# A first stage in another order: x turned before it is modulated, and half of the modulation sums on TensorE

## The chip, the cores and the metric

One core of a Trainium2 chip. The time is the device time of one execution in microseconds (us); of several runs the median is given. The engines are called PE (TensorE; PEld its weight loads), DVE (VectorE), ACT (ScalarE), POOL (GpSimd) and SP (SyncE, which only issues transfers).

## The reference

A transformer block for 1024 tokens of width 1024, all float32. What matters here is its beginning:

```python
c_act = jax.nn.silu(c)
mod = c_act @ w_mod[l] + b_mod[l]
sh1, sc1, gt1, sh2, sc2, gt2 = jnp.split(mod, 6, axis=-1)
h = modulate(rmsnorm(x, g_mix[l]), sh1, sc1)      # rmsnorm(x)*g * (1 + sc1) + sh1
x = x + gt1[:, None, :] * token_mixers(h, cos, sin, w_in[l], ...)
h = modulate(rmsnorm(x, g_ffn[l]), sh2, sc2)
x = x + gt2[:, None, :] * hier_moe(h, ...)
```

w_mod is 1024 x 6144, so each of the six vectors is the product of silu(c), 1024 numbers, with a 1024 x 1024 piece (4 MB). The token mixers begin with h @ w_in; then come an indexer, two kinds of attention, and a mixture of 32 experts, which read 6 MB of weights each.

## The kernel before

The kernel is written as five programs, one per engine, which wait for one another by semaphores; the order on each engine is the order of its program. x is kept as eight tiles xs[t] of 128 tokens x 1024. The projections need it the other way round: hT[kt] holds 128 channels x 1024 tokens, kt = 0 to 7, normalized and modulated.

The first stage runs as follows. SP asks for five small vectors (L448 to L452: c, b_mod, g_mix, positions, b_forget, all counted by the semaphore c_in), for the first two 2 MB pieces of w_mod (L454), for the eight tiles of x (L456), then, as buffers come free, for two more pieces of w_mod (L459), for the narrow columns of w_in (L462, wsmall) and 512 wide ones (L464, wqi). DVE waits for c_in, prepares the angles of the rotary embedding (L1290 to L1305), makes sil = silu(c), and takes the sums of w_mod: `mod_sums(n)` adds up, for the 512 columns n, the eight row blocks times sil (L1317 and L1319, eight instructions), which leaves 128 partial sums per column in acc. ACT squares and sums each tile of x (L718), takes the root of all sums at once (L720), DVE scales the eight tiles (L1332). PE turns x by transposes (L950), four to a PSUM bank, sixteen banks in all, seven of them before it needs one back. After the seventh it makes the sums over the partitions: 16 products of a 128 x 128 piece of acc with one column of ones (L956), which give shift and scale, one column of PSUM for each 128 channels. DVE adds b_mod and g_mix (L1337 to L1339: sh1, a1). Only then can a bank leave PSUM: ACT and DVE take the banks in turn and apply a1 and sh1 on the way (L729, L1351). When all sixteen are out, PE projects tile after tile (`project`: L966, 208 columns, then L971, 512 columns) and DVE takes the eight remaining `mod_sums`, one after each tile's rotary embedding.

Each float32 product stands in the trace as two matmul instructions; a transpose is one. POOL fills the constants first (invf, wm, ident, upper, ones; L605 to L616), the semaphores freq_ok and consts; PE waits for consts, DVE for freq_ok.

## Time and profile before

| | us |
|---|---|
| runs (3) | 1920.46, 1921.70, 1925.42 |
| median | 1921.7 |
| the profiled execution, its own time | 1920.38 |
| its span | 1918.1 |
| PE busy | 1682.2 |
| DVE busy | 983.1 |
| ACT busy | 494.1 |
| POOL busy | 193.8 |

The span runs from the first to the last instruction of the profiled execution; 2.3 us of its own time lie around it. Mean granted clock of PE is 0.957 of full speed. In the rows below, "idle before" names what ended an engine's wait; PEclk of 1.00 is 2.4 GHz, of 0.50 is 1.2 GHz; a DMA share of 1.0 means that all sixteen DMA engines were busy.

### The profile page before, as it was taken

The page shows a single profiled execution, that of the slowest core. Times are in us where ns is not written, and L with a number is a line of the kernel's source. Part 1 is how long each engine was busy: PE and PEld are TensorE (multiplying, and loading weights), DVE is VectorE, ACT ScalarE, POOL GpSimd, SP SyncE. Part 2 cuts the span into 40 slices and gives each one's busy share as a digit, 9 for nine tenths or more (in the row PEclk, how much of TensorE's full clock was granted, in tenths as well). Part 3 has the DMA queues.
Part 4 walks back from the last instruction along what each step waited for, and adds up shares of the span by engine and source line. Part 5 has one row for each costly group of instructions (what it writes and reads, how often), then busy time and mean ns, then how long its engine had stood idle before and what let it go on. Part 6 is the DMA issues. An engine that isn't in the chain of part 4 may idle for free.

```text
span 1918.1 us, 22810 instructions
## 1 busy us (share of the span) xinstructions
PE 1682.2 (88%) x7893; PEld 868.9 (45%) x7894; DVE 983.1 (51%) x1928; ACT 494.1 (26%) x976; POOL 193.8 (10%) x370
## 2 busy tenths in 40 slices
PE   1997899999998886999999995799888999899991
PEld 0662366565544453676665553333222333333330
DVE  6477558888887564556555435223222233233334
ACT  2116254554545563110110111111111111111112
POOL 0010000000000000000000000122211222222220
PEclk9898999999999998999999997799998999999996
DMA  8552311010001002112114516599999973779967
GB/s 281 187 208 77 142 35 45 23 44 1 1 1 56 1 1 66 34 33 66 33 33 162 225 66 248 195 394 391 405 405 405 400 270 61 268 271 397 355 223 279
DMA packets 114582, 325.52 MB, mean 170 GB/s; under 512 B 15240, under 2 KB 53128, under 8 KB 89936
## 3 DMA queue, kind: packets, MB, share of 16 engines
q1 hardware_dynamic: 102768, 296.79, 40.8%
q0 software_dynamic: 11744, 27.79, 6.1%
q8 instruction: 44, 0.72, 0.2%
q14 instruction: 26, 0.21, 0.0%
HBM read 293.33 MB, written 31.23 MB: 169 GB/s over the span
## 4 chain that ended last, share of the span: by engine, by line
PE 76%; DVE 8%; DMA 8%; ACT 4%; issue 3%; SPq 1%; DVEq 0%; ACTq 0%; POOLq 0%; POOL 0%
PE ps L1216 17%; PE ps L1156 9%; PE ps L1234 8%; PE ps L1017 6%; PE ps L1145 6%; PE ps L1170 5%; DMA arena<-in_w_e_up_dram 5%; PE ps L1042 3%; PE ps L1023 3%; PE ps L1093 3%; PE ps L971 3%; PE ps L1067 3%; PE ps L1053 2%; DVE arena L1401 2%; PE ps L1210 2%
## 5 line engine op out<-in xcount | busy, mean ns | idle before, releaser
L1216 PE MATMUL ps<-arena 128*64 128x512 f32 x1632 | 387.0, 618 | 39.1 <-DMA arena<-in_w_e_up_dram 27.6
L1743 DVE COPY arena<-ps 128x256 f32<-128x256 f32 x51 | 21.6, 424 | 425.5 <-ACT arena L902 425.5
L1216 PEld LDWEIGHTS ps<-arena 128*64 128x64 f32 x1632 | 118.5, 141 | 261.6 <-issue 254.5
L1234 PE MATMUL ps<-arena 128*64 128x512 f32 x816 | 186.3, 598 | 0.5 <-ACT arena L906 0.5
L1156 PE MATMUL ps<-rounded 128*128 128x512 f32 x768 | 183.3, 398 | 0.0
L1419 DVE TENSOR_SCALAR_CACHE_REDUCE arena<-arena,small 128x384 bf16<-128x384 f32 (+2 forms) x204 | 182.0, 939 | 0.0
L1156 PEld LDWEIGHTS ps<-rounded 128*128 128x128 f32 x768 | 144.3, 188 | 36.5 <-issue 7.7
L703 POOL DMA_INDIRECT sum_rows<-arena,ones x51 | 81.4, 1595 | 467.9 <-DVE arena L1765 459.1
L1145 PE MATMUL ps<-arena 128*128 128x512 f32 x256 | 115.3, 604 | 13.2 <-DVEq L1589 13.2
L1017 PE MATMUL ps<-arena 128*128 128x512 f32 x256 | 116.7, 610 | 4.8 <-ACT arena L766 3.4
L1067 PE MATMUL ps<-arena 128*64 128x128 f32 x1152 | 96.1, 287 | 26.3 <-ACT arena L800 22.8
L906 ACT ACTIVATE arena<-ps 128x256 f32<-128x256 f32 x51 | 19.5, 383 | 371.9 <-PE ps L1225 371.9
L1482 DVE CUSTOM_DVE_ANT_0 arena<-ps,arena 128x896 f32<-128x896 f32 (+7 forms) x128 | 91.7, 753 | 46.0 <-PE ps L1042 45.9
L1170 PE MATMUL ps<-arena 128*128 128x512 f32 x256 | 112.0, 595 | 2.0 <-DMA arena<-in_w_out_dram 2.0
L800 ACT ACTIVATE arena<-ps 128x512 f32<-128x512 f32 (+1 forms) x160 | 85.1, 551 | 84.3 <-PE ps L1053 83.8
L1595 DVE RECIPROCAL arena<-arena 128x1024 f32<-128x1024 f32 x16 | 104.8, 6553 | 0.5
L787 ACT ACTIVATE arena<-arena,small 128x896 f32<-128x896 f32 (+7 forms) x128 | 97.8, 768 | 19.9 <-DVE small L1482 19.9
L1234 PEld LDWEIGHTS ps<-arena 128*64 128x64 f32 x816 | 54.2, 136 | 93.9 <-issue 87.9
L1067 PEld LDWEIGHTS ps<-arena 128*64 128x64 f32 x1152 | 60.0, 136 | 74.0 <-ACT arena L800 45.9
L1042 PE MATMUL ps<-arena 64*128 64x512 f32 (+3 forms) x384 | 80.8, 526 | 12.3 <-DVE small L1482 11.6
L1053 PE MATMUL ps<-ident,arena 128*128 128x128 f32 x576 | 89.0, 287 | 0.0
L1748 DVE RECIPROCAL arena<-arena 128x256 f32<-128x256 f32 x51 | 89.0, 1745 | 0.0
(267 smaller groups left out, 1915.4 us busy)
## 6 DMA issues: line engine op xcount, KB each, us to landing
arena<-in_w_e_gate_dram SPq DMA_DIRECT2D x32, 2048.0 KB, 15.0
arena<-in_w_e_up_dram SPq DMA_DIRECT2D x32, 2048.0 KB, 20.1
arena<-in_w_e_down_dram SPq DMA_DIRECT2D x32, 2048.0 KB, 15.6
arena<-in_w_mod_dram SPq DMA_DIRECT2D x12, 2048.0 KB, 8.9
arena<-in_w_in_dram SPq DMA_DIRECT2D x33, 512.0 KB, 4.6
arena<-in_x_dram SPq DMA_DIRECT2D x16, 512.0 KB, 12.3
arena<-sum_rows SPq DMA_DIRECT2D x16, 512.0 KB, 10.6
sum_rows<-arena SPq DMA_DIRECT2D x2, 2304.0 KB, 16.5
```

The costliest lines, as they stand in the source:

```text
L787: act.activation(buf, buf, ACT.Exp, bias=nmax[:, u:u + 1], scale=-1.0, accum_out=rs[:, u:u + 1]).then_inc(p_done, 1)
L1017: m = pe.matmul(ps[:, 7, :], wB[j][:, kt, :], hT[:, kt, half * 512:(half + 1) * 512], start=kt == 0, stop=kt == KT - 1)
L1042: m = pe.matmul(ps[:, 2 * z + a // 512, 0:e - a], q[half, b * P:(b + 1) * P], k[half, a:e], start=True, stop=True)
L1053: m = pe.transpose(ps[:, 4 + k % 2, (2 * i + z) * P:(2 * i + z + 1) * P], logits(n)[z][:, kb * P:(kb + 1) * P], ident[:])
L1067: m = pe.matmul(ps[z * HD:(z + 1) * HD, 6, 0:P], v, pT_of(n, g)[:, (2 * i + z) * P:(2 * i + z + 1) * P], start=kb == 0, stop=kb == b)
L1145: m = pe.matmul(ps[:, 4 * half + 2 + g, :], w[2 + g][:, kt, :], oT[g][kt][:, tok], start=kt == 0, stop=kt == 3)
L1156: m = pe.matmul(ps[:, 4 * half + g, :], a, b, start=kt == 0 and k == 0, stop=kt == KT - 1 and k == 2)
L1170: m = pe.matmul(ps[:, 2 * (t % 2) + n, :], mT[:, kt, t * P:(t + 1) * P], wout[:, kt, n * 512:(n + 1) * 512], start=kt == 0, stop=kt == KT - 1)
L1216: m = pe.matmul(ps[o * TB:(o + 1) * TB, 2, 0:2 * FQ].rearrange("p (j n) -> p j n", j=2), xT[:, k % NX, k // NX * TB:(k // NX + 1) * TB], w ...
L1234: m = pe.matmul(ps[o * TB:(o + 1) * TB, 5, 0:DQ], hidT[:, k % NH_T, k // NH_T * TB:(k // NH_T + 1) * TB], w_dn[c][:, k, o * DQ:(o + 1) * D ...
L1419: chain.up(dve.tensor_scalar(junk[b % 2][:, 0:WB[B0 + b]], scb[b], thr(b), None, op, ALU.add, accum_out=cnt[:, b:b + 1]))
L1595: link(dve.reciprocal(e, e))
```

## The change

The five small vectors are asked for by POOL, ahead of its constants, and no longer by SP. SP asks for x first, then for all four pieces of w_mod (four buffers instead of two, so no waits), then for wsmall and wqi. ACT and DVE take x tile by tile: square, mean, root, reciprocal, scaling; PE turns each scaled tile (eight transposes in two banks), and ACT and DVE copy the two banks to hT without modulation. After the last tile ACT takes the exponential for sil. The sums for n = 1 and 3 stay on DVE; those for n = 0 and 2 are made by PE alone, as products of w_mod's 128 x 128 pieces with the column sil[kt], eight to a sum. With sh1 and a1 known, ACT (kt = 0, 3, 6) and DVE (the others) modulate hT in place, and PE's first projection waits for one kt after the other. The counts of acc_ok fall by two everywhere, and mod2's first loads wait for modp_ok too.

```diff
         xs = at(37, 8 * U, [TT, D])
-        wslot = [at(8, 4 * U, [KT, 512]), at(12, 4 * U, [KT, 512])]
+        mod1 = [at(u, 4 * U, [KT, 512]) for u in (16, 21, 25, 30)]
         wsmall = at(8, KT * P_N, [KT, P_N])
-        wqi = wslot[1]
+        wqi = at(12, 4 * U, [KT, 512])
+        sq_out = [at(45 + z, U) for z in range(2)]
         acc = [at(49, U), at(50, U)] + [at(45 + j, U) for j in range(4)]
...
         def _(sp):
-            sp.dma_start(cT, c.rearrange("o (t p) -> p (o t)", p=P), allow_slow_non_contiguous=True).then_inc(c_in, 16)
-            sp.dma_start(bmod, b_mod[0, 0:2 * D].rearrange("(t p) -> p t", p=P), allow_slow_non_contiguous=True).then_inc(c_in, 16)
-            sp.dma_start(gmix, g_mix[0].rearrange("(t p) -> p t", p=P), allow_slow_non_contiguous=True).then_inc(c_in, 16)
-            sp.dma_start(posi, positions[0].rearrange("(t p) -> p t", p=P), allow_slow_non_contiguous=True).then_inc(c_in, 16)
-            sp.dma_start(bfb, b_forget[0:1, :].to_broadcast([P, NH])).then_inc(c_in, 16)
-            for n in range(2):
-                sp.dma_start(wslot[n], w_mod_v[:, :, n * 512:(n + 1) * 512]).then_inc(mod_in[n], 16)
             for t in range(TT):
                 sp.dma_start(xs[:, t, :], x_v[t]).then_inc(x_in[t], 16)
-            for n in range(2, 4):
-                sp.wait_ge(acc_ok, n - 1)
-                sp.dma_start(wslot[n % 2], w_mod_v[:, :, n * 512:(n + 1) * 512]).then_inc(mod_in[n % 2], 16)
-            sp.wait_ge(acc_ok, 3)
+            for n in range(4):
+                sp.dma_start(mod1[n], w_mod_v[:, :, n * 512:(n + 1) * 512]).then_inc(mod_in[n], 16)
             for a, b, n in ((C_KI, P_KI, 72), (C_KA, P_KA, 128), (C_F, P_F, NH)):
                 sp.dma_start(wsmall[:, :, b:b + n], w_in_v[:, :, a:a + n], allow_slow_non_contiguous=True).then_inc(wi_in[0], 16)
-            sp.wait_ge(acc_ok, 4)
             sp.dma_start(wqi, w_in_v[:, :, C_QI:C_QI + 512]).then_inc(wi_in[1], 16)
             sp.wait_ge(xt_ps, 16)
+            sp.wait_ge(modp_ok, 1)
             for n in range(4, 12):
                 if n >= 6:
-                    sp.wait_ge(acc_ok, n - 1)
+                    sp.wait_ge(acc_ok, n - 3)
                 sp.dma_start(mod2[n % 2], w_mod_v[:, :, n * 512:(n + 1) * 512]).then_inc(mod_in[n % 2], 16)
...
                 if j == 2:
-                    sp.wait_ge(acc_ok, 12)
+                    sp.wait_ge(acc_ok, 10)
                 sp.dma_start(wB[j], w_in_v[:, :, (C_QB, C_KB, C_VB)[j]:(C_QB, C_KB, C_VB)[j] + P]).then_inc(wb_in[j], 16)
...
 
+            pool.dma_start(cT, c.rearrange("o (t p) -> p (o t)", p=P), allow_slow_non_contiguous=True).then_inc(c_in, 16)
+            pool.dma_start(posi, positions[0].rearrange("(t p) -> p t", p=P), allow_slow_non_contiguous=True).then_inc(c_in, 16)
+            pool.dma_start(bmod, b_mod[0, 0:2 * D].rearrange("(t p) -> p t", p=P), allow_slow_non_contiguous=True).then_inc(c_in, 16)
+            pool.dma_start(gmix, g_mix[0].rearrange("(t p) -> p t", p=P), allow_slow_non_contiguous=True).then_inc(c_in, 16)
+            pool.dma_start(bfb, b_forget[0:1, :].to_broadcast([P, NH])).then_inc(c_in, 16)
             for j in range(HALF):
...
         def _(act):
-            act.wait_ge(c_in, 80)
-            act.activation(sil, cT, ACT.Exp, scale=-1.0).then_inc(silu_e, 1)
-            for t in range(TT):
+            def square(t):
                 act.wait_ge(x_in[t], 16)
                 if t >= 2:
                     act.wait_ge(ssq_ok, t - 1)
-                act.activation(relu[t % 2], xs[:, t, :], ACT.Square, accum_out=ssq[:, t:t + 1]).then_inc(ssq_ok, 1)
-            act.wait_ge(ms_ok, 1)
-            act.activation(rstd, ssq, ACT.Sqrt).then_inc(sqrt_ok, 1)
+                act.activation(sq_out[t % 2], xs[:, t, :], ACT.Square, accum_out=ssq[:, t:t + 1]).then_inc(ssq_ok, 1)
+
+            def turned_x(t):
+                act.wait_ge(xt_ps, 2 * t + 1)
+                act.activation(hT[:, 0:4, t * P:(t + 1) * P], ps[:, 2 * t % 6, :].rearrange("p (j m) -> p j m", j=4), ACT.Copy).then_inc(xt_act, 1)
+
+            square(0)
+            for t in range(TT):
+                if t + 1 < TT:
+                    square(t + 1)
+                act.wait_ge(ms_ok, t + 1)
+                act.activation(rstd[:, t:t + 1], ssq[:, t:t + 1], ACT.Sqrt).then_inc(sqrt_ok, 1)
+                if t >= 1:
+                    turned_x(t - 1)
+            turned_x(TT - 1)
+            act.wait_ge(c_in, 80)
+            act.activation(sil, cT, ACT.Exp, scale=-1.0).then_inc(silu_e, 1)
             act.wait_ge(ang_ok, 1)
...
             act.wait_ge(mod1_ok, 2)
-            for n in range(0, 16, 2):
-                act.wait_ge(xt_ps, n + 1)
-                kt, half = n // 2, n % 2
-                act.activation(hT[:, kt, half * 512:(half + 1) * 512], ps[:, n % 7, :], ACT.Identity,
-                               bias=sh1[:, kt:kt + 1], scale=a1[:, kt:kt + 1]).then_inc(xt_act, 1)
+            act.wait_ge(xt_dve, TT)
+            for kt in (0, 3, 6):
+                act.activation(hT[:, kt, :], hT[:, kt, :], ACT.Identity, bias=sh1[:, kt:kt + 1], scale=a1[:, kt:kt + 1]).then_inc(xt_act, 1)
 
...
                 pe.wait_ge(xn_ok, t + 1)
-            for n in range(16):
-                kt, half = n // 2, n % 2
-                if n >= 7:
-                    pe.wait_ge(xt_act if (n - 7) % 2 == 0 else xt_dve, (n - 7) // 2 + 1)
-                for j in range(4):
-                    t = 4 * half + j
-                    m = pe.transpose(ps[:, n % 7, j * P:(j + 1) * P], xs[:, t, kt * P:(kt + 1) * P], ident[:])
-                m.then_inc(xt_ps, 1)
-                if n == 6:
-
-                    pe.wait_ge(acc_ok, 4)
-                    for k in range(2 * KT):
-                        m = pe.matmul(ps[:, 7, k:k + 1], acc[k // KT][:, (k % KT) * P:(k % KT + 1) * P], ones[:, 0:1],
-                                      start=True, stop=True)
-                    m.then_inc(modp_ok, 1)
-            pe.wait_ge(xt_act, 8)
-            pe.wait_ge(xt_dve, 8)
+                for h in range(2):
+                    if t >= 3:
+                        pe.wait_ge((xt_act, xt_dve)[h], t - 2)
+                    for j in range(4):
+                        kt = 4 * h + j
+                        m = pe.transpose(ps[:, (2 * t + h) % 6, j * P:(j + 1) * P], xs[:, t, kt * P:(kt + 1) * P], ident[:])
+                    m.then_inc(xt_ps, 1)
+
+            pe.wait_ge(sil_ok, 1)
+            for n in (0, 2):
+                pe.wait_ge(mod_in[n], 16)
+                for k in range(4 * n, 4 * n + 4):
+                    for kt in range(KT):
+                        m = pe.matmul(ps[:, 7, k:k + 1], mod1[n][:, kt, k % 4 * P:(k % 4 + 1) * P], sil[:, kt:kt + 1],
+                                      start=kt == 0, stop=kt == KT - 1)
+            for n in (1, 3):
+                pe.wait_ge(acc_ok, 1 + n // 2)
+                for k in range(4 * n, 4 * n + 4):
+                    m = pe.matmul(ps[:, 7, k:k + 1], acc[k // KT][:, (k % KT) * P:(k % KT + 1) * P], ones[:, 0:1], start=True, stop=True)
+            m.then_inc(modp_ok, 1)
 
...
                 for kt in range(KT):
+                    if t == 0 and kt % 3 == 0:
+                        pe.wait_ge(xt_act, TT + 1 + kt // 3)
+                    elif t == 0:
+                        pe.wait_ge(xt_dve, TT + kt - kt // 3)
                     pe.matmul(ps[:, t % 2, 0:P_N], hT[:, kt, t * P:(t + 1) * P], wsmall[:, kt, :],
...
 
-            dve.wait_ge(silu_e, 1)
-            link(dve.tensor_scalar(sil, sil, 1.0, None, ALU.add))
-            link(dve.reciprocal(sil, sil))
-            link(dve.tensor_tensor(sil, sil, cT, ALU.mult))
-
             def mod_sums(n):
 
-                w = wslot[n % 2] if n < 4 else mod2[n % 2]
-                dve.wait_ge(mod_in[n % 2], 16 * (n // 2 + 1))
+                w = mod1[n] if n < 4 else mod2[n % 2]
+                dve.wait_ge(mod_in[n if n < 4 else n % 2], 16 if n < 4 else 16 * ((n - 4) // 2 + 2))
                 a = acc[n // 2][:, (n % 2) * 512:(n % 2 + 1) * 512]
...
 
-            mod_sums(0)
+            def turned_x(t):
+                dve.wait_ge(xt_ps, 2 * t + 2)
+                dve.tensor_copy(hT[:, 4:8, t * P:(t + 1) * P], ps[:, (2 * t + 1) % 6, :].rearrange("p (j m) -> p j m", j=4)).then_inc(xt_dve, 1)
+
+            def mean(t):
+                dve.wait_ge(ssq_ok, t + 1)
+                dve.tensor_scalar(ssq[:, t:t + 1], ssq[:, t:t + 1], 1.0 / D, EPS, ALU.mult, ALU.add).then_inc(ms_ok, 1)
+
+            mean(0)
+            for t in range(TT):
+                if t + 1 < TT:
+                    mean(t + 1)
+                dve.wait_ge(sqrt_ok, t + 1)
+                link(dve.reciprocal(rstd[:, t:t + 1], rstd[:, t:t + 1]))
+                dve.tensor_scalar(xs[:, t, :], xs[:, t, :], rstd[:, t:t + 1], None, ALU.mult).then_inc(xn_ok, 1)
+                if t >= 1:
+                    turned_x(t - 1)
+            dve.wait_ge(silu_e, 1)
+            link(dve.tensor_scalar(sil, sil, 1.0, None, ALU.add))
+            link(dve.reciprocal(sil, sil))
+            dve.tensor_tensor(sil, sil, cT, ALU.mult).then_inc(sil_ok, 1)
+            turned_x(TT - 1)
+            dve.wait_ge(sil_ok, 1)
             mod_sums(1)
-
-            dve.wait_ge(ssq_ok, TT)
-            dve.tensor_scalar(ssq, ssq, 1.0 / D, EPS, ALU.mult, ALU.add).then_inc(ms_ok, 1)
-            dve.wait_ge(sqrt_ok, 1)
-            link(dve.reciprocal(rstd, rstd))
-            for t in range(TT):
-                dve.tensor_scalar(xs[:, t, :], xs[:, t, :], rstd[:, t:t + 1], None, ALU.mult).then_inc(xn_ok, 1)
-            mod_sums(2)
             mod_sums(3)
...
             dve.scalar_tensor_tensor(a1, a1, 1.0, gmix, ALU.add, ALU.mult).then_inc(mod1_ok, 1)
+
+            dve.wait_ge(mod1_ok, 2)
+            dve.wait_ge(xt_act, TT)
+            for kt in range(KT):
+                if kt % 3:
+                    dve.tensor_scalar(hT[:, kt, :], hT[:, kt, :], a1[:, kt:kt + 1], sh1[:, kt:kt + 1], ALU.mult, ALU.add).then_inc(xt_dve, 1)
 
...
             link(dve.tensor_copy(cos2[:, :, 1, :], cos2[:, :, 0, :]))
-
-            dve.wait_ge(mod1_ok, 2)
-            for n in range(1, 16, 2):
-                dve.wait_ge(xt_ps, n + 1)
-                kt, half = n // 2, n % 2
-                dve.tensor_scalar(hT[:, kt, half * 512:(half + 1) * 512], ps[:, n % 7, :], a1[:, kt:kt + 1],
-                                  sh1[:, kt:kt + 1], ALU.mult, ALU.add).then_inc(xt_dve, 1)
 
```

Left out are the declarations of semaphores and three more places where a wait for acc_ok 12 becomes one for 10.

On POOL, at the start of its program: these rows stood there before (small is where invf and wm lie).

```order
L605 MEMSET small 128x1 x8
L607 MEMSET small 128x1 x6
L609 MEMSET ident 128x128
L610 MEMSET upper 128x128
L611 MEMSET ones 128x128
L614 ISA [waits pool_chain]
L614 AFFINE_SELECT ident<-ident 128x128
L616 AFFINE_SELECT upper<-upper 128x128
```

And these stand there now, with the five transfers ahead of the constants.

```order
L596 DMA small<-in_c_dram 128x8x1
L597 DMA small<-in_positions_dram 128x8x1
L598 DMA small<-in_b_mod_dram 128x16x1
L599 DMA small<-in_g_mix_dram 128x8x1
L600 DMA small<-in_b_forget_dram 128x8
L602 MEMSET small 128x1 x8
L604 MEMSET small 128x1 x6
L606 MEMSET ident 128x128
L607 MEMSET upper 128x128
L608 MEMSET ones 128x128
L611 ISA [waits pool_chain]
L611 AFFINE_SELECT ident<-ident 128x128
```

Everything that POOL does in this stage has moved behind the transfers: freq_ok, for which DVE waits, and consts, for which PE waits.

On DVE, from the last angle step on, before (ssq, rstd and sil lie in small, xs, acc and the buffers of w_mod in arena):

```order
L1305 TENSOR_SCALAR arena<-arena 128x64 [waits dve_chain]
L1308 TENSOR_SCALAR small<-small 128x8 [waits silu_e]
L1309 RECIPROCAL small<-small 128x8 [waits dve_chain]
L1310 TENSOR_TENSOR small<-small 128x8 [waits dve_chain]
L1317 TENSOR_SCALAR arena<-arena,small 128x512 [waits mod_in0,dve_chain]
L1319 SCALAR_TENSOR_TENSOR arena<-arena,small 128x512 [waits dve_chain] x7
L1317 TENSOR_SCALAR arena<-arena,small 128x512 [waits mod_in1]
L1319 SCALAR_TENSOR_TENSOR arena<-arena,small 128x512 [waits dve_chain] x7
L1328 TENSOR_SCALAR small<-small 128x8 [waits ssq_ok]
L1330 RECIPROCAL small<-small 128x8 [waits sqrt_ok]
L1332 TENSOR_SCALAR arena<-arena,small 128x1024 [waits dve_chain]
L1332 TENSOR_SCALAR arena<-arena,small 128x1024 x7
```

And now:

```order
L1319 TENSOR_SCALAR arena<-arena 128x64 [waits dve_chain]
L1339 TENSOR_SCALAR small<-small 128x1 [waits ssq_ok] x2
L1346 RECIPROCAL small<-small 128x1 [waits sqrt_ok]
L1347 TENSOR_SCALAR arena<-arena,small 128x1024 [waits dve_chain]
L1339 TENSOR_SCALAR small<-small 128x1 [waits ssq_ok]
L1346 RECIPROCAL small<-small 128x1 [waits sqrt_ok]
L1347 TENSOR_SCALAR arena<-arena,small 128x1024 [waits dve_chain]
L1335 COPY arena<-ps 128x4x128 [waits xt_ps]
L1339 TENSOR_SCALAR small<-small 128x1 [waits ssq_ok]
L1346 RECIPROCAL small<-small 128x1 [waits sqrt_ok]
```

The scaling of the first tile comes right behind the angles instead of behind two sums, in rounds of a tile each; sil has moved behind the eighth tile.

On PE, from the last transposes of x to the last one-column product, now (small is sil, ps the PSUM):

```order
L956 MATMUL ps<-ident,arena 128x128 [waits xt_act,xn_ok]
L956 MATMUL ps<-ident,arena 128x128 x3
L956 MATMUL ps<-ident,arena 128x128 [waits xt_dve]
L956 MATMUL ps<-ident,arena 128x128 x3
L964 MATMUL ps<-small,arena 128x1 [waits mod_in0,sil_ok]
L964 MATMUL ps<-small,arena 128x1 x31
L964 MATMUL ps<-small,arena 128x1 [waits mod_in2]
L964 MATMUL ps<-small,arena 128x1 x31
L969 MATMUL ps<-ones,arena 128x1 [waits acc_ok]
L969 MATMUL ps<-ones,arena 128x1 x3
L969 MATMUL ps<-ones,arena 128x1 [waits acc_ok]
L969 MATMUL ps<-ones,arena 128x1 x3
```

Of these L964 is new, 64 products; of L969's kind there were 16 and are 8.

## Rows read from the trace of the kernel before

**Rows 1.** The page: busy time by engine, and the chain's shares by engine.

```profile
PE 1682.2 (88%) x7893; PEld 868.9 (45%) x7894; DVE 983.1 (51%) x1928; ACT 494.1 (26%) x976; POOL 193.8 (10%) x370
...
PE 76%; DVE 8%; DMA 8%; ACT 4%; issue 3%; SPq 1%; DVEq 0%; ACTq 0%; POOLq 0%; POOL 0%
```

**Rows 2.** The chain that ended last, 0 to 150 us: start, us, what.

```profile
14.53 14.84 DMA arena<-in_x_dram
...
49.60 7.00 PE ps L956 x32
...
57.93 5.51 PE ps L950 x32
...
64.82 3.05 PE ps L966 x16
67.87 6.87 PE ps L971 x16
```

**Rows 3.** Stretches: us, busy (instructions) of PE, PEld, DVE, ACT, POOL, clock, DMA share, GB/s.

```profile
20.00:30.00 10.00, 0.00 (x0) 0.00 (x0) 5.48 (x8) 8.65 (x15) 0.00 (x0) 1.00 1.03 406
43.00:48.00 5.00, 0.00 (x0) 0.00 (x0) 4.79 (x7) 0.00 (x0) 0.00 (x0) 1.00 0.72 168
50.00:56.00 6.00, 6.00 (x29) 6.00 (x30) 0.00 (x0) 0.00 (x0) 0.00 (x0) 0.50 0.90 318
57.00:61.00 4.00, 3.07 (x15) 3.04 (x16) 3.87 (x10) 3.56 (x5) 0.00 (x0) 0.50 0.00 0
62.00:63.00 1.00, 1.00 (x12) 1.00 (x10) 0.81 (x1) 0.83 (x2) 0.00 (x0) 1.00 0.00 0
1166.00:1168.00 2.00, 2.00 (x20) 1.98 (x18) 1.38 (x2) 0.33 (x1) 0.00 (x0) 1.00 0.00 0
1178.00:1181.00 3.00, 3.00 (x16) 3.00 (x15) 0.00 (x0) 0.00 (x0) 0.00 (x0) 0.50 1.02 434
```

**Rows 4.** Timeline of DVE, 0 to 63 us: start, us, engine, line, operation, idle before.

```profile
7.88 0.17 DVE L1290 CAST small<-small 128x8 f32<-128x8 int32 x1 [7.88 <-DMA small<-in_b_forget_dram]
...
10.52 0.20 DVE L1305 TENSOR_SCALAR arena<-arena 128x64 f32<-128x64 f32 x1
...
32.34 5.39 DVE L1332 TENSOR_SCALAR arena<-arena,small 128x1024 f32<-128x1024 f32 x8
...
38.16 5.47 DVE L1319 SCALAR_TENSOR_TENSOR arena<-arena,small 128x512 f32<-128x512 f32 x7
...
57.81 3.79 DVE L1351 TENSOR_SCALAR arena<-ps,small 128x512 f32<-128x512 f32 x5
```

**Rows 5.** Timeline of SP's queue, 0 to 5 us.

```profile
4.58 0.89 SPq L452 DMA_DIRECT2D small<-in_b_forget_dram  x1
```

**Rows 6.** Timeline of ACT, 20 to 76 us.

```profile
20.43 1.06 ACT L718 ACTIVATE arena<-arena 128x1024 f32<-128x1024 f32 x1 [12.35 <-DMA arena<-in_x_dram]
...
21.71 1.06 ACT L718 ACTIVATE arena<-arena 128x1024 f32<-128x1024 f32 x1
...
30.57 1.28 ACT L720 ACT_TABLE_LOAD   x1
31.86 0.21 ACT L720 ACTIVATE small<-small 128x8 f32<-128x8 f32 x1
...
75.07 0.59 ACT L741 ACTIVATE arena<-ps 128x512 f32<-128x512 f32 x1
```

**Rows 7.** Timeline of PE: the first transposes, and router products about 1170 us.

```profile
37.88 4.84 PE L950 MATMUL ps<-ident,arena 128*128 128x128 f32 x28 [37.88 <-DVE arena L1332]
...
1166.89 1.87 PE L1188 MATMUL ps<-arena 128*128 128x36 f32 x16
...
1173.84 3.47 PE L1188 MATMUL ps<-arena 128*128 128x36 f32 x16
```

**Rows 8.** A group on POOL, shapes apart: xcount, busy, mean ns, idle before.

```profile
L673 POOL DMA_INDIRECT arena<-h_rows,ones x55 | 55.5, 1009 | 43.6 <-POOL ones L670 43.6
```

**Rows 9.** Source line L673: its transfers from issue to landing.

```profile
DMA to landing us min/median/max: 3.4/8.6/10.6
```

10 lines of the change are left out of this document (5 added, 5 removed).

## The prediction

> **What bounds the kernel now.** The page comes first: TensorE (PE) is busy 88% of the span and carries 76% of the chain that ended last [rows 1]. A share over the whole span does not say what ends this stage, so the second view is that chain in order of time [rows 2]. It reads: the load of x (14.84 us) to 29.4 us, the eight scalings of x on VectorE (DVE) and two modulation sums there [rows 4], at 49.60 us sixteen one-column products on PE (7.0 us, 32 instructions), the last transposes, and at 64.82 us the first projection: 3.05 us of 208-column and 6.87 us of 512-column products, over at 74.74 us. Before 64.82 us nobody can project; after it PE works tile after tile, and what follows hangs on that end. So the time of this change is the shift of 74.74 us, one for one: I know of no slack behind it that would absorb a shift, since the later weight loads are issued by events of the same chain. The third view is the stretches with the granted clock [rows 3], then come the timelines of DVE, SP, ACT and PE, and the groups of POOL's own transfers.
>
> **What goes.** x no longer stands behind 4 MB of w_mod and does not wait for the sums; the 16 transposes of a half need no modulation vector. Two of the four sums leave DVE. All 12.6 MB of x and w_mod plus 2.9 MB of w_in are now asked for without a wait: at 406 GB/s [rows 3] that is 38 us, so mod1[3] is in by about 36 us and w_in by 44 us (with some 4 us of latency). Each is in before it is needed below, so these loads cost nothing; the cover is the PE work that runs until after 60 us.
>
> **What comes, step by step.** Call t the time at which the five small vectors (c_in) have landed. It was 7.88 us [rows 4], the last having been issued by SP at 4.58 us [rows 5].
>
> 1. DVE waits for t ahead of everything, as before, and its angle work takes 2.8 us (7.88 to 10.72) [rows 4]. In the old order this stood beside loads. Now the scaling of tile 0 is queued behind it, and PE's first transpose waits for that. The tile loop starts at t + 2.8.
>
> 2. The loop is bounded by ScalarE (ACT), which per tile does a square (1.28 us from one to the next), a root (0.2) and a copy of 512 columns from PSUM (0.6) [rows 6], with about 0.1 for handing over: 2.2 us. DVE has two small steps of 0.2, a scaling of 0.7 (5.39/8) and a copy from PSUM of 0.8 (3.79/5) = 1.9 us per tile [rows 4] and PE eight transposes of at most 0.17 us (5.51/32) [rows 2] = 1.4 us, so both hide beside ACT. x comes at 1.3 us a tile and hides too. Seven rounds are 15.4 us, the last tile's own scaling, transposes and copy 0.7 + 0.6 + 0.6 = 1.9 us: 17.3 us. ACT then loads a table (1.28) and takes the exponential (0.2) [rows 6]; DVE's three small steps are 0.6 us. So sil is ready at t + 2.8 + 17.3 + 1.5 + 0.6 = **t + 22.2**.
>
> 3. PE now makes 64 one-column products from w_mod itself (for n = 0 and 2) and 8 from the two sums left: 72 products, 144 instructions. The 32 of before took 7.0 us, 219 ns each [rows 2], at the lower of the clock's two levels, 0.50 = 1.2 GHz [rows 3]. 144 x 0.219 = **31.5 us**, where 7.0 stood. A weight load per product sets this pace: router products of 36 columns take 3.47/16 = 217 ns at the lower level and 1.87/16 = 117 ns at 1.00, 2.4 GHz [rows 3, 7]. So the bounds are 16.8 us and 31.5 us. I take 31.5: in the stretch 50 to 56 us the clock stood at 0.50 although PE was busy with such products all the time, and again at 1178 to 1181 us with 36 columns, whereas transposes from 57.93 us on brought it to 1.00 by 62 us [rows 2, 3]. DVE's two sums (6 us each, 5.47 us of it for the seven longer steps [rows 4]) hide beside the first 28 us.
>
> 4. From the last product to the first projection: 0.5 us for the two vectors, 1.1 us for ACT's first 1024-wide modulation, as its square is [rows 6]. The other seven pieces are ready at 0.7 to 1.1 us steps while PE works. The first projection then starts at the lower clock. Transposes needed about 4 us to bring it up (57.93 to 62) [rows 2, 3], so about 2 us are lost on the 9.9. Together 0.5 + 1.1 + 9.9 + 2.0 = **13.5 us**; before, 56.6 to 74.74 was 18.1 us.
>
> Sum: the first projection ends at t + 22.2 + 31.5 + 13.5 = t + 67.2. Against 74.74 the change is **t - 7.5 us**. Even with the old t = 7.88 nothing is gained: the early transposes are paid back by the one-column products. The outcome now hangs on t, at one for one.
>
> **How large t is.** The five vectors leave SP for POOL's queue. c, positions, b_mod and g_mix go as single 4-byte elements: 1024, 1024, 2048 and 1024 of them; last comes b_forget with 128 rows. The trace of before has no direct transfer from POOL. The nearest row is the gather of L673: 1.0 us of POOL for 128 rows [rows 8]. Lower bound: 1.0 us each, so 4.0 us ahead of the last. Upper bound: the cost grows with the elements, 1009/128 = 7.9 ns each, x 5120 = 40 us. I take 2.0 us each, 8 us, nearer the lower end, since a good part of 1009 ns must be fixed. From issue to landing a gather takes 3.4 us at best and 8.6 in the median [rows 9], the latter with SP's weight loads beside it; SP's x and w_mod are beside it here, so 8.6. With POOL's start at 0.8 us, t = 0.8 + 8 + 8.6 = 17.4 us, and the change is 17.4 - 7.5 = **+9.9 us**. The memsets of ident and ones also stand behind these transfers on POOL, but they end before t + 2.8 and cost nothing then. The profiled execution took 1920.4 us, 1.3 us under the median of 1921.7; the shift is the same for both, so I forecast 1921.7 + 9.9 = 1931.6 us.
>
> **Rivals.** *Quick landing (0.24).* Each transfer takes POOL 1.0 us and lands in 3.4 us: t = 0.8 + 4.0 + 3.4 = 8.2 us, the change is +0.7 us, 1922.4 us. Everything with t under 13.3 us belongs here, since 0.3% (5.8 us), about what a measurement of this kernel can tell from no change, is reached at that t. For it: 3.4 us occurs in the trace [rows 9]. Against it: the engines move 400 GB/s from 8 us on [rows 3]. The Trainium skill, "DMA: Bandwidth & Descriptors", section on the anatomy of a transfer from POOL, puts a transfer at about 2.0 us plus its bytes at 436 GB/s; by that, an estimate, t would be some 7 us and the change about -0.5 us.
>
> *Elements are dear (0.14).* 7.9 ns for each of 5120 elements gives t = 0.8 + 40 + 8.6 = 49 us and +42 us, 1964 us; if small pieces instead take turns with SP's rows on the engines until SP's 38 us of loads are through, t is about 40 us and the change +33 us. For it: each vector is all single elements, 5120 pieces in all where a gather has 128. The rules at the end of the same page of the skill say that a strided last dimension costs a descriptor per element. No row here shows what POOL pays for one.
>
> *The other side: the clock holds (0.10).* If PE's clock is up after the transposes and the one-column products keep it, they cost 16.8 us instead of 31.5, and the 2.0 us at the projection go too: -16.7, with t = 17.4 a change of -6.8 us, 1914.9 us. It becomes faster than before once more than 9.9/16.7 = 60% of that comes. For it: the clock stood at 1.00 until 48 us although the transposes had stopped at 42.7 us [rows 3, 7]. Against it: 7 us of the same products without a rise, and about 3 us lie between the last transpose and the first product. What I grant is some us of full clock at the start, up to 4.5 us (5 us hold 43 instructions at 117 ns, which else take 9.4).
>
> **How the numbers follow.** Forecast, t from 13.3 to 34 us: 0.52, likeliest 1931.6 us. The range runs from the quick landing with up to 4.5 us of clock, 1922.4 - 4.5 = 1918, to 1948 us, where t is 34 us (four transfers of 6 us); that leaves out most of the dear elements and the fully held clock, about 0.2. Slower by over 0.3%: 0.52 + 0.14, less 0.04 in which a partly held clock brings it under = 0.62. Within: 0.24 + 0.04 - 0.01 = 0.27. Faster: 0.10 plus 0.01 of the quick landing with some clock = 0.11.
>
> **What would show it.** In the changed profile: POOL's five transfers with their durations and the first DVE instruction at t (17 us; under 13 or over 34 refutes my price); ACT's rounds of 2.2 us; sil ready 22 us after t; 128 instructions of one column in 28 us at granted clock 0.50 (15 us at 1.00 if the last rival holds); the first projection over at t + 67, and everything behind it shifted by the same amount. I am wrong in kind, not in size, if the projection starts well before 60 us, or if the shift of its end is not found again in the total.

## The result, and the profile after

| | before | after |
|---|---|---|
| runs compared | 20 | 20 |
| median, us | 1923.01 | 1927.25 |
| the profiled execution, its own time, us | 1920.38 | 1924.9 |
| its span, us | 1918.1 | 1923.2 |
| mean granted clock | 0.957 | 0.951 |

The ratio is 1.0021, with a 95% interval of 1.0012 to 1.0030: the changed kernel is slower by 4.2 us (2.3 to 5.8). I had forecast +9.9 us. The direction is right, the forecast is 2.4 times what was measured, and 4.2 us lie within the 0.3% that I had called no change.

The chain that ended last, after, 0 to 80 us (start, us, what):

```profile
1.36 1.12 POOL small L596
2.48 0.94 POOL small L597
3.42 1.14 POOL small L598
4.56 0.83 POOL small L599
5.39 7.37 DMA small<-in_b_forget_dram
12.78 0.19 DVE small L1304
...
33.06 25.62 PE ps L964 x128
58.68 3.43 PE ps L969 x16
...
62.61 1.25 ACT arena L737
63.86 0.14 issue
64.00 5.64 PE ps L980 x16
69.64 6.87 PE ps L985 x16
```

It has the shape that I had drawn: the small vectors, then the tile loop, then the one-column products, then the projection. The vectors have landed at t = 12.78 us. The last line ends at 76.51 us, where [rows 2] ended at 74.74: only 1.8 us later.

ACT's timeline, after, one round of the tile loop and its end:

```profile
20.38 1.05 ACT L713 ACTIVATE arena<-arena 128x1024 f32<-128x1024 f32 x1
21.32 0.19 ACT L713 ACTIVATION_READ_ACCUMULATOR arena<-arena 128x1 f32 x1
21.42 0.19 ACT L724 ACTIVATE small<-small 128x1 f32<-128x1 f32 x1
21.87 0.60 ACT L717 ACTIVATE arena<-ps 128x512 f32<-128x512 f32 x1 [0.27 <-PE ps L956]
22.37 1.05 ACT L713 ACTIVATE arena<-arena 128x1024 f32<-128x1024 f32 x1
...
30.86 1.28 ACT L729 ACT_TABLE_LOAD   x1
32.16 0.21 ACT L729 ACTIVATE small<-small 128x8 f32<-128x8 f32 x1
```

From one square to the next it is 1.99 us here; the five squares from 18.67 to 25.82 us give 1.79 us on average. PE's stretches, after (us, busy of PE, PEld, DVE, ACT, POOL, clock, DMA share, GB/s):

```profile
28.00:34.50 6.50, 3.62 (x29) 3.15 (x29) 4.06 (x11) 4.38 (x7) 0.00 (x0) 1.00 1.05 387
34.00:35.00 1.00, 1.00 (x12) 1.00 (x11) 0.93 (x3) 0.09 (x1) 0.00 (x0) 1.00 1.04 385
35.00:36.00 1.00, 1.00 (x8) 1.00 (x7) 0.96 (x2) 0.00 (x0) 0.00 (x0) 0.56 1.04 385
36.00:58.00 22.00, 22.00 (x105) 22.00 (x104) 9.12 (x13) 0.00 (x0) 0.00 (x0) 0.50 0.53 167
58.00:62.00 4.00, 4.00 (x20) 4.00 (x19) 0.00 (x0) 0.00 (x0) 0.00 (x0) 0.50 0.00 0
64.00:69.00 5.00, 5.00 (x15) 4.87 (x16) 2.95 (x8) 2.12 (x2) 0.00 (x0) 0.50 1.04 383
69.00:72.00 3.00, 3.00 (x9) 1.62 (x8) 0.00 (x0) 0.00 (x0) 0.00 (x0) 0.96 1.04 384
```

The stream of one-column products began, at 33.06 us, with the clock at 1.00. Some 2 us later it was at 0.50 and stayed there to 69 us, while PE was busy except for 1.90 us ahead of the projection. That answers to the stretches at 50 and 1178 us in [rows 3].

How the clock had come up is seen in the pace of the transposes, not in the clock's column, which reads 1.00 from the span's start on, with PE idle too:

```profile
17.05 3.65 PE L956 MATMUL ps<-ident,arena 128*128 128x128 f32 x16 [17.05 <-DVE arena L1347]
...
22.65 1.09 PE L956 MATMUL ps<-ident,arena 128*128 128x128 f32 x8 [0.38 <-DVE arena L1347]
```

The first sixteen take 228 ns each, those from 22.65 us on 137 ns each.

Past the stage the distance between the two profiles is not constant: +1.8 us through 150 us, +0.7 from 240 to 1040 us, +2.2 at 1190 us and +4.3 where the experts end, at 1876 us. So part of the measured difference is not made in the stage that was changed. The step down from +1.8 to +0.7 is the clock again: the sixteen 512-column instructions that start at 206 us before (L1017) and at 208 us after (L1031) take 9.79 and 8.83 us, at a mean granted clock of 0.51 and 0.77 between 206 and 212 us.

### The profile page after: what moved, and what is told of

It is laid out like the page before. It is cut to its first block, busy times and chain, and to the rows that moved or that the text cites. A ratio compares the mean times of both kernels' runs of the same rounds, so it can differ in the third digit from the quotient of the medians.

```text
span 1923.2 us, 23053 instructions
## 1 busy us (share of the span) xinstructions
PE 1706.6 (89%) x8005; PEld 890.3 (46%) x8006; DVE 976.5 (51%) x1931; ACT 497.7 (26%) x987; POOL 198.7 (10%) x375
## 2 busy tenths in 40 slices
DMA packets 109434, 325.56 MB, mean 169 GB/s; under 512 B 10088, under 2 KB 47976, under 8 KB 84784
## 4 chain that ended last, share of the span: by engine, by line
PE 76%; DVE 8%; DMA 7%; ACT 5%; issue 3%; SPq 1%; POOL 0%; DVEq 0%; ACTq 0%; POOLq 0%
PE ps L1230 17%; PE ps L1170 9%; PE ps L1248 8%; PE ps L1031 6%; PE ps L1159 6%; DMA arena<-in_w_e_up_dram 5%; PE ps L1184 4%; PE ps L1056 3%; PE ps L1037 3%; PE ps L1107 3%; PE ps L985 3%; PE ps L1081 3%; PE ps L1067 2%; DVE arena L1423 2%; PE ps L1224 2%
## 5 line engine op out<-in xcount | busy, mean ns | idle before, releaser
L1031 PE MATMUL ps<-arena 128*128 128x512 f32 x256 | 115.8, 606 | 4.4 <-ACT arena L773 3.0
L1056 PE MATMUL ps<-arena 64*128 64x512 f32 (+3 forms) x384 | 80.7, 525 | 12.3 <-DVE small L1504 11.5
```

Of the source, the lines that this page charges most:

```text
L1031: m = pe.matmul(ps[:, 7, :], wB[j][:, kt, :], hT[:, kt, half * 512:(half + 1) * 512], start=kt == 0, stop=kt == KT - 1)
L1056: m = pe.matmul(ps[:, 2 * z + a // 512, 0:e - a], q[half, b * P:(b + 1) * P], k[half, a:e], start=True, stop=True)
```

## The experiments

Four questions: what t is worth, what the one-column products are worth, whether a shift of the stage reaches the total, and where the rest arises. Medians are set against those of before in the same comparison, 1922.81 to 1923.57 us. "Stage end" is the start of the second tile's projection in PE's timeline: 74.57 us before, 76.34 after; it lies 0.17 us ahead of the end of the first projection.

### The vectors from SP, ahead of x

```diff
+            sp.dma_start(cT, c.rearrange("o (t p) -> p (o t)", p=P), allow_slow_non_contiguous=True).then_inc(c_in, 16)
...
+            sp.dma_start(bfb, b_forget[0:1, :].to_broadcast([P, NH])).then_inc(c_in, 16)
             for t in range(TT):
                 sp.dma_start(xs[:, t, :], x_v[t]).then_inc(x_in[t], 16)
...
-            pool.dma_start(cT, c.rearrange("o (t p) -> p (o t)", p=P), allow_slow_non_contiguous=True).then_inc(c_in, 16)
...
-            pool.dma_start(bfb, b_forget[0:1, :].to_broadcast([P, NH])).then_inc(c_in, 16)
```

> The changed kernel, but the five small vectors are issued by SP again, ahead of x; nothing else differs. My theory: DVE and with it the tile loop start when the vectors have landed, so t goes back from 12.8 to about 7.9 us and all that follows moves up by 4.9 us; the first projection ends at about 71.6 us (76.5 in the changed kernel, 74.7 before), and the total is 3 us under the kernel before. Rival 1 (x is the bound): x now lands later by the same 5 us, ACT waits for it, the loop ends no earlier and the total stays 4 us above before. Rival 2 (POOL's own transfers cost something later on as well, since the total rose by 4.2 us where the first projection ended only 1.8 us later): the total falls by more than the 4.9 us, to 5 us or more under before.

Median 1925.16 us, ratio 1.0008 [0.9997, 1.0019]; stage end 75.66. DVE and ACT in this kernel:

```profile
7.83 0.17 DVE L1304 CAST small<-small 128x8 f32<-128x8 int32 x1 [7.83 <-DMA small<-in_b_forget_dram]
```

```profile
9.53 1.06 ACT L713 ACTIVATE arena<-arena 128x1024 f32<-128x1024 f32 x1 [7.46 <-DMA arena<-in_x_dram]
```

t fell by 4.95 us, but the first square, at 4.40 us in the changed kernel, now starts at 9.53: x has become what the loop waits for. PE's first transpose is only 2.4 us earlier (14.61 against 17.05). So t is on the path, but only until x takes its place. Of these 2.4 us the stage end keeps 0.7, since the first 128 one-column instructions take 27.47 us instead of 25.62: the clock was at 0.50 from the start of their stream on.

### The tile loop ahead of the wait for the vectors

```diff
-            dve.wait_ge(c_in, 80)
-            link(dve.tensor_copy(pos, posi))
...
-            dve.tensor_scalar(angr, angr, pi, -pi, ALU.min, ALU.max).then_inc(ang_ok, 1)
...
                 dve.tensor_scalar(xs[:, t, :], xs[:, t, :], rstd[:, t:t + 1], None, ALU.mult).then_inc(xn_ok, 1)
                 if t >= 1:
                     turned_x(t - 1)
+            dve.wait_ge(c_in, 80)
+            link(dve.tensor_copy(pos, posi))
...
+            dve.tensor_scalar(angr, angr, pi, -pi, ALU.min, ALU.max).then_inc(ang_ok, 1)
```

On POOL the five transfers stand behind the constants here.

> The changed kernel, but DVE takes the loop over the eight tiles first and waits for the small vectors (and does its angle work) only behind it; POOL fills its constants ahead of the five transfers, because TensorE now needs ident early. My theory: the loop no longer hangs on t but on x, which lands by about 17 us; sil is ready at about 25 us instead of 33, and the first projection ends near 68.5 us, 6 us under before, with the total 6 us under before. Rival (the one-column products wait for something else, such as w_mod): they start no earlier than 33 us and nothing is gained on the changed kernel.

Median 1920.64 us, ratio 0.9987 [0.9976, 0.9997]; stage end 69.54, 6.8 us ahead of the changed kernel. The first transpose starts at 9.70 us and the products at 26.30. DVE then waits for w_mod (1.75 and 4.87 us), which costs nothing, since PE is still in its own stream. Waiting for t ahead of the loop had cost the changed kernel these 6.8 us; the angle work stays on DVE's way to sil (22.91 to 25.73 us), but much of it now stands beside ACT's table load. The stage end is 1.2 us later than I had expected (69.7 for 68.5 us at the end of the projection), and the total missed by more: 2.3 us under before (0.6 to 4.6) instead of 6.

### All four sums on DVE, and three of them

```diff
-            for n in (0, 2):
+            for n in (0,):
                 pe.wait_ge(mod_in[n], 16)
...
-            for n in (1, 3):
-                pe.wait_ge(acc_ok, 1 + n // 2)
+            for i, n in enumerate((1, 2, 3)):
+                pe.wait_ge(acc_ok, i + 1)
...
+            mod_sums(2)
```

This is the version with three sums on DVE (the counts of acc_ok behind them rise by one); in the one with four the first loop is gone.

> The changed kernel, but all four modulation sums are taken by DVE, and TensorE keeps only the 16 products with ones; the new order of x stays. My theory: 219 ns for each of 128 added instructions is dearer than the two sums that DVE is spared. DVE ends its fourth sum at about 57.7 us, the last four products follow in 1.8 us, so the vectors are there at about 59.5 us where the changed kernel has 62.1; first projection over at about 73.9 us, total 2.6 us under the changed kernel and about 1 us (with a further 2 us, if the changed kernel's excess behind the stage is real) around before. Rival: the products on TensorE are what the change gains by, DVE is the bound, and without them the stage ends later than in the changed kernel.

> The changed kernel, but the split of the four sums is 3 on DVE and 1 on TensorE instead of 2 and 2. My theory: DVE's three sums end at about 51.7 us, TensorE is through with its 64 instructions at about 45 us and with the earlier products by 49, and the last four products end at 53.4 us against 62.1: the first projection is over near 67.8 us, 8.7 us earlier than in the changed kernel and 7 us earlier than before; total 7 us under before. If one microsecond of this stage is not worth one of the total, the total falls by clearly less.

Four on DVE: 1924.89 us, ratio 1.0005 [0.9995, 1.0016], stage end 72.95. Three: 1915.80 us, ratio 0.9962 [0.9949, 0.9976], stage end 67.94. The first projection ends at 73.1 and 68.1 us, for 73.9 and 67.8 expected; the rival for four sums, a later end than in the changed kernel, is refuted. PE in the second:

```profile
33.20 13.24 PE L964 MATMUL ps<-small,arena 128*128 128x1 f32 x64 [2.41 <-DVE small L1353]
46.31 3.55 PE L969 MATMUL ps<-ones,arena 128*128 128x1 f32 x16
51.53 1.86 PE L969 MATMUL ps<-ones,arena 128*128 128x1 f32 x8 [1.67 <-DVE arena L1328]
```

A sum costs PE 13.2 us, or DVE 5.9 us (0.48 and 5.47, one behind the other) and PE another 1.9 us for the sum over the partitions. With three on DVE the two engines end together, 1.67 us apart; with two, DVE is idle for 15.8 us at the end while PE streams; with four, PE is idle between sums. The changed kernel's even split is what makes it slow.

### The two edits together

The code is that of the last two diffs together.

> The two edits that gained alone, together: the tile loop ahead of the wait for the small vectors and of the angle work, POOL's constants ahead of its transfers, and three of the four sums on VectorE. Theory (the two gains are on one path and add as far as VectorE allows): e_loop_free had its exponential's result at 26.3 us, 6.7 us ahead of the changed kernel; from there VectorE's three sums take 18 us when w_mod is in, but they wait for w_mod, whose fourth block lands at about 38 us. So the sums end at about 46 us, the 16 products and the modulation bring the first projection's end to about 63 to 66 us, 2 to 5 us ahead of e_three_dve (67.94). Total 1911 to 1914 us, if the stages behind carry it. Rival (w_mod's arrival or VectorE is the bound already): the end stays within 1 us of 67.94 and the total within 2 us of 1915.8.

Median 1911.87 us, ratio 0.9940 [0.9927, 0.9954], stage end 61.62: 14.7 us ahead of the changed kernel, 6.3 ahead of three sums on DVE alone. The two gains, 6.8 and 8.4 us alone, nearly add; the projection's end, 61.8 us, came 1.2 us earlier than the range I had expected. This is faster than both kernels, by 11.4 us than before. What bounds it now is DVE: PE waits 3.83 us for DVE's last sum, and DVE had itself waited 1.54 and 0.56 us for w_mod.

### Filling the array to hold the clock

Products that nobody reads, into an unused bank: of 128x256 in bf16, after every two one-column products, in the changed kernel and in the best one; of 128x128 in float32, after every one-column product; and the latter in the best kernel, but in the gaps in which PE waits.

```diff
                         m = pe.matmul(ps[:, 7, k:k + 1], mod1[n][:, kt, k % 4 * P:(k % 4 + 1) * P], sil[:, kt:kt + 1],
                                       start=kt == 0, stop=kt == KT - 1)
+                        if kt % 2 == 1:
+                            pe.matmul(ps[:, 6, 0:2 * P], ones[:, 0:P // 2].bitcast(BF16), ones[:].bitcast(BF16), start=True, stop=True)
```

> The changed kernel, with a bf16 dummy product of 128x256 after every two of the 128 one-column instructions' pairs (32 dummies, into a PSUM bank that nobody reads). Theory A (the one-column stream is slow only because TensorE's clock goes to its lower level in it, and it goes there because that stream leaves the array almost idle): the granted clock stays at 1.00 through the stream; the 144 instructions cost 144 x 0.117 = 17 us instead of 29.0, the dummies add 32 x 0.11 = 3.5 us, the projection no longer starts at the lower clock (2.6 us less); the end of the first projection moves from 76.5 to about 65 to 67 us if nothing else becomes late. VectorE's two sums (about 12 us beside it) must still be in time, they end at about 46 us. Theory B (the clock falls whatever fills the gaps, or the pace of the stream is set by something else): the stream takes 29 us plus the dummies at the lower clock, 7 us more, total up by 7 us.

> As e_best, with 16 dummy products of 128x256 in bf16 among the 64 remaining one-column instructions of w_mod on TensorE. In e_best that stream (13 us) is shorter than VectorE's three sums (18 us), so TensorE waits anyway. Theory A (the stream is hidden; the dummies help only the clock at the projection, if at all): within 2 us of e_best. Theory B (the clock is held until the projection): up to 3 us faster than e_best.

> The changed kernel, with one full float32 product of 128x128 (as the transposes, 0.137 us each at the full clock) after every pair of the 128 one-column instructions: 64 of them, into a bank that nobody reads. The bf16 products of e_warm2 did not hold the clock. Theory A (a dense enough fill holds it): granted clock 1.00 throughout, the stream takes 144 x 0.117 + 64 x 0.137 = 25.6 us, less than the 29.0 of the changed kernel, and the projection starts at full clock: its end at about 71 to 73 us. Theory B (nothing holds it while weights are loaded for one column each): 29 + 64 x 0.27 = 46 us, end at about 94 us, total up by 17 us.

None held it: in all three the clock was at 0.50 within some 2 us of the stream's start. Medians 1925.80 us (1.0017 [1.0005, 1.0029], stage end 78.95), 1913.91 us (0.9949 [0.9936, 0.9962], stage end 62.83) and, with the float32 products and from two runs only, 1954.47 us (1.0162 [1.0138, 1.0187], stage end 103.89). The bf16 fill itself cost next to nothing: four one-column instructions and one fill take 0.88 us, four alone 0.86 (16 in 3.43). So theory B's 7 us did not come either; the stage ended 2.6 us later than in the changed kernel, and 1.2 us later than in the best one. The stretches of the last one:

```profile
30.00:35.00 5.00, 2.58 (x23) 2.35 (x22) 2.60 (x7) 3.79 (x6) 0.00 (x0) 1.00 1.04 387
35.00:40.00 5.00, 5.00 (x27) 5.00 (x27) 4.79 (x8) 0.00 (x0) 0.00 (x0) 0.54 1.10 339
...
60.00:70.00 10.00, 10.00 (x48) 10.00 (x49) 0.00 (x0) 0.00 (x0) 0.00 (x0) 0.50 0.01 2
```

Theory B's sign is right and its size (46 us, total +17) is too small. I had counted a fill as one instruction of 0.27 us, and a float32 product is two: a one-column pair with its fill takes 0.85 us, where the pair alone takes 0.43, and the stage ended 27.6 us later than in the changed kernel (64 times 0.42 are 27).

```diff
             for i, n in enumerate((1, 2, 3)):
+                if i == 2:
+                    for _ in range(14):
+                        pe.matmul(ps[:, 6, 0:P], ones[:], ones[:], start=True, stop=True)
                 pe.wait_ge(acc_ok, i + 1)
...
             m.then_inc(modp_ok, 1)
+            for _ in range(6):
+                pe.matmul(ps[:, 6, 0:P], ones[:], ones[:], start=True, stop=True)
```

> e_best, with float32 products of 128x128 nobody reads in the two gaps in which TensorE waits there: 14 ahead of the last sum's wait (3.83 us idle in e_best at 42.57 us; 0.27 us each at the lower clock), 6 behind the last one-column product (1.90 us idle ahead of the projection at 50.16 us). Theory (dense work in those gaps brings the clock up before the projection starts): its first 16 instructions take 3.05 us instead of 4.76, the end of the first projection moves from 61.6 to about 60 us, total 1.7 us less than e_best. Rival: the clock rises when it did, at 52.9 us, and the total stays within 1 us of e_best.

Median 1911.34 us, ratio 0.9938 [0.9922, 0.9954], stage end 61.90: the same as without. PE in this kernel:

```profile
39.73 3.55 PE L972 MATMUL ps<-ones,arena 128*128 128x1 f32 x16
43.14 6.22 PE L969 MATMUL ps<-ones 128*128 128x128 f32 x28
49.20 0.95 PE L972 MATMUL ps<-ones,arena 128*128 128x1 f32 x8
...
52.05 3.15 PE L985 MATMUL ps<-arena 128*128 128x208 f32 x16 [0.45 <-ACT arena L737]
```

```profile
48.00:50.00 2.00, 2.00 (x15) 2.00 (x15) 0.00 (x0) 0.00 (x0) 0.00 (x0) 0.72 0.00 0
```

The clock did come up here, at about 49 us by the last line (a stretch, columns as above): the eight one-column instructions take 0.95 us instead of 1.86 and the projection's first sixteen 3.15 instead of 4.76. But here too I had taken a product for one instruction: 14 are 28, 6.2 us instead of 3.8, and the sum that had waited at 46.40 us starts at 49.20. What the clock gave, the fill took. The same products raise the clock in a row, and do not hold it when they take turns with one-column ones.

### Does a shift reach the total?

The kernel before, with scalings on DVE ahead of the shift vector that nobody reads, 13 and 4 of them, and the changed kernel with 6 shorter ones:

```diff
             dve.wait_ge(modp_ok, 1)
+            for _ in range(13):
+                link(dve.tensor_scalar(acc[2], acc[0], 1.0, None, ALU.mult))
             dve.tensor_tensor(sh1, ps[:, 7, 0:KT], bmod[:, 0:KT], ALU.add).then_inc(mod1_ok, 1)
```

> The kernel before, with 13 chained scalings of 128x1024 put on VectorE right behind its wait for the 16 products (the scalings of x are 0.67 us each in the profile of before, so about 9 us). Nothing else moves. Theory (a shift of the first projection reaches the total one for one, as the prediction has it): the end of the first projection goes from 74.74 to about 83.7 us and the total up by about 9 us, ratio 1.0047. Rival (later stages absorb or add on their own, because the kernel is not stiff): the first projection is 9 us later, but the total moves by less than 5 us or by more than 12 us.

> The kernel before with 4 chained scalings of 128x1024 on VectorE ahead of the modulation vectors, as e_delay had 13: about 3.1 us later, near where the changed kernel stands at the end of its first projection. Theory (the missing 2 us belong to the changed order): the median is 3.1 us above before, within 1 us. Rival (a shift of this size costs more than itself by the clock of later stages, whoever makes it): 4.5 to 6 us above before, and in the profile losses at the places where the changed kernel lost, near 636 us and 1175 us.

> The changed kernel with 6 chained scalings of 128x512 on VectorE at the same place, about 3 us. Theory (a fixed loss in the changed order): 3 us more than the changed kernel, 7 to 8.5 us above before. Rival (the loss depends on where the shift puts the later stages): the distance to the changed kernel is off 3 us by over 1.5 us either way.

The 13 scalings: stage end 84.72 (+10.2), median 1933.34 us, +10.1 (ratio 1.0053 [1.0040, 1.0065]). The 4: stage end 77.22 (+2.7), median 1925.64, +2.1 (1.0016 [1.0003, 1.0030]). A shift of the kernel before does reach the total one for one, within 0.6 us, and a small one costs nothing more. The changed kernel with 6: stage end 79.58 (+5.0), median 1929.40, +5.8 (1.0028 [1.0016, 1.0040]); I had expected 7 to 8.5 for a fixed loss.

### Both kernels once more

> The kernel before once more, unchanged, for a second profile. Theory (the stages behind the first scatter by a few us with the places at which TensorE's clock is lower, from one execution to the next): the end of the first projection is within 0.5 us of 74.74 again, while later marks differ by 1 to 3 us from the first profile, and the time at the lower clock in the expert stage differs by some us from 70.5. Rival (later stages are the same in every execution, so that a difference there belongs to a kernel): all marks to the end within 0.5 us of the first profile.

> The changed kernel once more, unchanged. Theory (the 2.3 us that its first profile loses behind the first stage are scatter or a small mean loss through the clock): the first projection ends within 0.5 us of 76.51, the distance from there to the end differs by 1 us or more from the first profile's, and the median is 1 to 5 us above that of before. Rival (a fixed loss behind the first stage): again +2 us or so against before by 1180 us and +4 us at the end, at the same places.

Medians 1923.16 us (1.0002 [0.9992, 1.0013]) and 1928.26 us (1.0026 [1.0016, 1.0036]). Before: every mark up to 1250 us is within 0.5 us of the first profile, and the experts then end 2.0 us later. So between these two profiles of that kernel only the expert stage differs. The changed kernel differs at the start already:

```profile
14.60 0.17 DVE L1304 CAST small<-small 128x8 f32<-128x8 int32 x1 [14.60 <-DMA small<-in_b_forget_dram]
```

t is 14.60 us instead of 12.78, with POOL's five transfers at the same times within 0.01 us: the last one landed after 9.2 us instead of 7.4. The stage ends at 77.89, 1.6 us later than in the first profile (I had expected 0.5 at most); t reaches it nearly one for one. A second difference lies at 620 to 700 us, here for before, the two profiles of the changed kernel, and the kernel with the loop ahead, in that order:

```profile
620.00:700.00 80.00, 64.75 (x555) 39.66 (x553) 46.85 (x139) 47.87 (x112) 0.00 (x0) 1.00 0.03 13
```

```profile
620.00:700.00 80.00, 64.77 (x558) 40.16 (x559) 46.51 (x138) 48.64 (x114) 0.00 (x0) 1.00 0.04 14
```

```profile
620.00:700.00 80.00, 66.51 (x549) 41.25 (x547) 44.92 (x131) 47.02 (x106) 0.00 (x0) 0.96 0.07 24
```

```profile
620.00:700.00 80.00, 67.14 (x526) 41.65 (x523) 43.28 (x127) 45.04 (x103) 0.00 (x0) 0.91 0.00 1
```

The two with the clock below 1.00 lose time there: 3.0 us between 590 and 704 us in the repeated profile of the changed kernel, 5.5 us in the one with the loop ahead. The code of that stretch is the same in all of them. It is no rare case: of the twelve profiles of kernels with the new order, eight lose 2.9 to 5.7 us there, at a granted clock of 0.91 to 0.96; the other four lose 0.5 us at most (three at 1.00, the float32 fill at 0.96). The four profiles with the order of before, delayed ones included, lose 0.6 us at most, at 1.00. Yet the first profile of the changed kernel is among those that lose nothing, so the order alone does not decide it.

All kernels together, shifts against before in us:

| kernel | stage end | median | difference |
|---|---|---|---|
| changed, first and second comparison | +1.8, +3.3 | +4.2, +5.5 | +2.4, +2.2 |
| vectors from SP | +1.1 | +2.2 | +1.1 |
| loop ahead | -5.0 | -2.3 | +2.7 |
| four sums on DVE | -1.6 | +2.0 | +3.6 |
| three sums on DVE | -6.6 | -7.1 | -0.5 |
| best; with bf16 fill; filled in the gaps | -13.0, -11.7, -12.7 | -11.4, -9.3, -11.5 | +1.6, +2.4, +1.2 |
| changed, bf16 fill | +4.4 | +2.6 | -1.8 |
| changed, float32 fill | +29.3 | +31.7 | +2.4 |
| changed, delayed | +5.0 | +5.8 | +0.8 |
| before, delayed by 13, by 4 | +10.2, +2.7 | +10.1, +2.1 | -0.1, -0.6 |

A kernel's stage end is from one profile, in which t alone can move it by 1.6 us, and its median carries some 1.5 us of uncertainty. The twelve differences with the new order run from -1.8 to +3.6 us, 1.5 on average.

## Why the prediction was right and wrong

**The bound, the path and the sign were right.** The stage end moved the way and by the path that I had drawn. Nothing is gained by the early transposes, because the one-column products on PE take it back; moving one sum off PE showed the reverse, 8.4 us at the stage end. That every us of the first projection's end is a us of the total held for the kernel before (+10.2 and +10.1).

**t was mis-sized, and this is the largest part of the miss.** I had 17.4 us; it was 12.8 and 14.6. The step that failed is POOL's price, "I take 2.0 us each, 8 us". The five transfers took POOL 1.12, 0.95, 1.18, 0.92 and 0.60 us, and the last started 4.0 us after the first, where I had 8. The lower bound, 1.0 us each [rows 8], was the value: 2048 elements cost 1.18 us and 1024 cost 0.92 to 1.12, so from 1024 on the elements hardly count, and I had leaned away from the nearest row on a guess that something must be added to it, though my own reason (a good part must be fixed) spoke for the row. Landing, 8.6 us from [rows 9], was 7.4 and 9.2: that term was right within what one execution differs from the next. POOL started at 1.36 us instead of 0.8. The estimate from the Trainium skill ("DMA: Bandwidth & Descriptors", anatomy of a transfer from POOL), some 7 us for t, was too low, since these transfers landed after 7.0 to 7.8 us with SP's loads beside them.

**The other terms of the sum**, predicted, then measured in the first and the second profile of the changed kernel: from t to sil 22.2, 20.3 and 20.0 us, because a round of ACT is 1.8 us and not 2.2 (its pieces overlap by about 0.1 us each; I had added busy times and handing over), which saves 2.9 us over seven rounds, of which the first tile's way to its transposes and the last tile's copies take back 0.8; the 144 one-column instructions 31.5, 29.1 and 29.8 us, since the first of them ran at the full clock (33.06 to about 35 us), which I had allowed for in a rival only; from there to the end of the projection 13.5, 14.4 and 13.6 us. With t these make 76.5 and 78.0 us. The form of the sum stands; only its sizes were off: -4.6 us for t, -2 for the loop, -2.4 for the stream, +0.9 for the rest make +1.8 out of +9.9. In the second profile t is only 2.8 us of the 6.6 us missed. One reading beside the sum was off as well: I had mod1[3] in by about 36 us, and DVE got it at 40.35; it cost nothing in the changed kernel, where PE was in its stream until 58.7 us.

**The step to the total did not hold as stated.** The two medians are 2.4 and 2.2 us further up than the two stage ends. My "one for one" is right for a pure delay of the kernel before, so this seems to belong to the kernels with the new order, by 1.5 us on average and unequally. Whether it is a fixed loss is not settled: the changed kernel delayed by 3 us more lost 0.8 us and not 2.3, but the two differ by no more than stage end and median are uncertain by. The rows at 620 to 700 us show one way, a lower clock in a stretch of unchanged code; that it makes up the whole was not shown, and why the delayed kernel before escapes it stays open. It is luck, then, that the total came as near to the forecast as +4.2: by its own path the forecast should be held against +1.8.

**The rivals.** Quick landing had the right side of t (under 13.3 us) in one profile of two, though for POOL's price and not for the landing. Dear elements is refuted. The held clock is refuted, but for the first 2 us of the stream it was held; that was worth some 2.4 us, of the 4.5 that I had granted.

## What to carry to other kernels

When a reduction is split between two engines, divide it by what each pays for a piece: here 13.2 us on PE against 5.9 us on DVE with 1.9 us on PE, so one to three and not two to two (some 19 us of PE beside 18 of DVE), which turned a loss of 4.2 us into a gain of 7.1. Keep a wait for late small data behind work that does not need it (6.8 us at the stage end here), and when a bound is the nearest row of the trace, take that row unless another one speaks against it.
